# A 31-tap depthwise convolution inside a two-block model: two taps change engine, and the weight stream changes order

## What is computed

```python
u = h @ w_pw1 + b_pw1
a, gt = jnp.split(u, 2, axis=-1)
u = a * jax.nn.sigmoid(gt)
u = lax.conv_general_dilated(u, w_dw[:, None, :], window_strides=(1,),      # 31 taps, one filter a channel
    padding=[(15, 15)], dimension_numbers=("NWC", "WIO", "NWC"), feature_group_count=1024) + b_dw
u = jax.nn.silu(layernorm(u, ln_g, ln_b))
return u @ w_pw2 + b_pw2
```

## Time and profile before

| | |
|---|---|
| time, median of 3 runs | 1968.42 us (1966.68 to 1971.39) |
| span of the profiled execution | 1969.0 us |
| convolution's taps on TensorE | 121.8 to 168.9 us |
| first pw2 matmul | 184.1 us |
| busy: PE, DVE, ACT, POOL | 1889.2, 1201.8, 953.6, 542.5 us |

### The profile page before, as it was taken

How to read it: one execution, slowest core, us unless ns; L and a number is a source line. 1 busy time by engine, 2 the same in 40 slices (tenths; PEclk the granted TensorE clock), 3 DMA queues, 4 the chain that set the end, 5 groups by cost and what they waited for, 6 DMA issues and landing times.

```text
span 1969.0 us, 36121 instructions
## 1 busy us (share of the span) xinstructions
PE 1889.2 (96%) x14718; PEld 1668.6 (85%) x14718; DVE 1201.8 (61%) x2440; ACT 953.6 (48%) x1709; POOL 542.5 (28%) x685
## 2 busy tenths in 40 slices
PE   6999999999998989999998999999999999999998
PEld 4855778888886857899987989999999899989997
DVE  4989763233338575655579675685648876567473
ACT  4314532232224477544456474565555556456464
POOL 1320010000001533000021222747373322374736
PEclk9999999999999999899999999999999999999999
DMA  9335442222224254655544444455554544545551
GB/s 358 128 108 206 151 150 96 97 97 97 97 97 171 86 193 175 211 182 182 183 160 175 142 136 160 165 168 172 194 182 152 174 148 133 168 150 178 187 178 59
DMA packets 84548, 307.24 MB, mean 156 GB/s; under 512 B 9376, under 2 KB 10656, under 8 KB 84128
## 3 DMA queue, kind: packets, MB, share of 16 engines
q1 hardware_dynamic: 84384, 304.94, 45.4%
HBM read 303.86 MB, written 1.05 MB: 155 GB/s over the span
## 4 chain that ended last, share of the span: by engine, by line
PE 82%; DVE 10%; ACT 5%; DMA 2%; issue 1%; SPq 0%; POOL 0%; DVEq 0%; ACTq 0%
PE pb L540 18%; PE pb L542 18%; PE pb L541 18%; PE pb L513 7%; PE pb L514 6%; PE pb L519 6%; DVE wlo L1897 2%; DMA raw<-wstream 2%; ACT whi L1237 1%; PE pb L591 1%; DVE Y L2146 1%; PE pb L765 1%; PE pb L924 1%; PE pb L1108 1%; PE pb L1121 1%
## 5 line engine op out<-in xcount | busy, mean ns | idle before, releaser
L540 PE MATMUL pb<-Hh,whi 128*128 128x256 f32 (+1 forms) x2304 | 701.8, 305 | 1.8 <-DVE SM L2480 1.6
L542 PE MATMUL pb<-Hh,wlo 128*128 128x256 f32 (+1 forms) x2304 | 694.6, 301 | 0.0
L541 PE MATMUL pb<-Hl,whi 128*128 128x256 f32 (+1 forms) x2304 | 694.6, 301 | 0.0
L1237 ACT ACTIVATE whi<-raw 128x1024 fp32r<-128x1024 f32 x468 | 489.3, 1054 | 318.1 <-PE pb L542 171.2
L2855 POOL TENSOR_TENSOR wlo<-raw,whi 128x256 fp32r<-128x256 f32 x576 | 434.9, 790 | 734.9 <-ACT whi L1237 733.9
L1897 DVE TENSOR_TENSOR wlo<-raw,whi 128x1024 fp32r<-128x1024 f32 x324 | 421.2, 1305 | 344.1 <-ACT whi L1237 343.7
L540 PEld LDWEIGHTS pb<-Hh,whi 128*128 128x128 f32 x2304 | 441.9, 192 | 22.9 <-DVE SM L2480 2.5
L541 PEld LDWEIGHTS pb<-Hl,whi 128*128 128x128 f32 x2304 | 442.2, 192 | 15.0
L542 PEld LDWEIGHTS pb<-Hh,wlo 128*128 128x128 f32 x2304 | 442.0, 192 | 15.0
L513 PE MATMUL pb<-Hh,whi 128*128 128x256 f32 (+1 forms) x528 | 161.2, 327 | 4.6 <-ACT Hh L1311 3.2
L514 PE MATMUL pb<-Hh,wlo 128*128 128x256 f32 (+1 forms) x528 | 158.8, 322 | 0.0
(11 more groups left out here) (333 smaller groups left out, 2952.6 us busy)
## 6 DMA issues: line engine op xcount, KB each, us to landing
raw<-wstream SPq DMA_DIRECT2D x572, 512.0 KB, 3.5
X<-xin SPq DMA_DIRECT2D x2, 1024.0 KB, 7.7
out<-X SPq DMA_DIRECT2D x8, 128.0 KB, 1.8
CON<-consts SPq DMA_DIRECT2D x1, 926.0 KB, 8.6
VEC<-vecs SPq DMA_DIRECT2D x1, 662.0 KB, 9.5
CON<-consts SPq DMA_DIRECT2D x1, 147.0 KB, 3.8
VEC<-vecs SPq DMA_DIRECT2D x1, 88.0 KB, 2.0
```

Of the source, the lines that this page charges most:

```text
L540: e.matmul(dst, hi, xh, start=k == 0, stop=False)
L541: e.matmul(dst, hi, xl, start=False, stop=False)
L542: i = e.matmul(dst, lo, xh, start=False, stop=k == kt - 1)
L1237: e.activation(whi[:, s % NPIECE, :], raw[:, p % NRAW, :], ACT.Copy).then_inc(sig("act_hi", ("hi", p)), 1)
```

## The change

The weight stream gets pw2's first four tiles before C's modulation weights, C has three groups and N three (before: four and two). TensorE does taps 0 to 28 only. Taps 29 and 30 of its four tiles are made by VectorE as a part of each tile, with the negative shift as the start value (`part_taps`), and TensorE adds each part with one round of the plain diagonal. The sums for the shift come before the taps, the spread after tap 3. C's bites are after taps 2, 5, 8, 11, 14 and 17, the transpose of its row after tap 23, N's first bite after tap 26. No low half of pw1 is GpSimd's any more, but those of pieces 18 and 19 are. VectorE evicts three of TensorE's tiles and squares one, ScalarE evicts the fourth. The two idle matmuls ahead of the spread go. The scaled tiles get the buffers 5 to 7 under a name of their own (`ct`), parts the buffers 4 to 7.

```diff
+CONV_PE = 29
...
-CHUNKS = [(i, min(CHUNK, CONVW - i)) for i in range(0, CONVW, CHUNK)]
+CHUNKS = [(i, min(CHUNK, CONV_PE - i)) for i in range(0, CONV_PE, CHUNK)]
...
-MODS = {"S0": (0, 2, 2), "S1": (1, 2, 2), "C": (4, 4, 1), "N": (8, 2, 1), "F": (10, 3, 1), "A": (13, 3, 1),
+MODS = {"S0": (0, 2, 2), "S1": (1, 2, 2), "C": (4, 3, 1), "N": (7, 3, 1), "F": (10, 3, 1), "A": (13, 3, 1),
...
-    mod("C")
-    run([("conv_w_pw2", (0,), m * 128) for m in range(8)], FIRST, then=["N"])
+    run([("conv_w_pw2", (0,), m * 128) for m in range(8)], FIRST, then=["C", "N"])
...
-            if tag == "pw1":
-                return s > 5 and s % 3 == 0
+            if s in (tile_turn["pw1", 15] + 3, tile_turn["pw1", 15] + 4):
+                return True
...
+            bank("norm", ("stat", "cs"), ("root", "cs"))
+            w.wait_ge(*on("cv", 0))
+            quarters("cs", Y[:, 0:512], 512, True, False, ("zsum", "cs"))
+            w.wait_ge(*on("cv", 1))
+            quarters("cs", Y[:, 512:1024], 512, False, True, ("sums", "cs"))
             w.wait_ge(*on("pad"))
-            for ct in range(4):
-                w.wait_ge(*on("u", 4 + ct))
-            for i_ in range(CONVW + 1):
+            for i_ in range(CONV_PE):
                 c, q = i_ // CHUNK, i_ % CHUNK
                 w.wait_ge(*on("dg", c))
-                if i_ == CONVW:
-                    w.wait_ge(*on("shift"))
                 dg = DG[:, c % 3, :, :, :]
                 for ct in range(4):
+                    if i_ == 0:
+                        w.wait_ge(*on("u", 4 + ct))
                     for r in range(4):
                         rows = slice(32 * r, 32 * r + 32)
-                        src = U[rows, 4 + ct, :, i_:i_ + T] if i_ < CONVW else two(slots.at("shift")[rows, :])
-                        i = e.matmul(two(got[r][32 * ct:32 * ct + 32, :]), dg[rows, ct, q, :], src, start=i_ == 0, stop=i_ == CONVW)
-                if i_ == CONVW:
-                    i.then_inc(sig("pe_conv", ("dgused", c), *[("conv", r) for r in range(4)]), 1)
-                elif q == CHUNK - 1:
+                        i = e.matmul(two(got[r][32 * ct:32 * ct + 32, :]), dg[rows, ct, q, :], U[rows, 4 + ct, :, i_:i_ + T],
+                                     start=i_ == 0, stop=False)
+                if i_ == CONV_PE - 1 or q == CHUNK - 1:
                     i.then_inc(sig("pe_conv", ("dgused", c)), 1)
-                if i_ % 3 == 2 and i_ < 30:
+                if i_ == 24:
+                    feed("N")
+                if i_ % 3 == 2 and (i_ < 18 or i_ == 26):
                     bite(1)
-                    if i_ == 29:
-                        mod_tr("mods")
-                if i_ == 8:
-                    bank("norm", ("stat", "cs"), ("root", "cs"))
-                    w.wait_ge(*on("cv", 0))
-                    quarters("cs", Y[:, 0:512], 512, True, False, ("zsum", "cs"))
-                    w.wait_ge(*on("cv", 1))
-                    quarters("cs", Y[:, 512:1024], 512, False, True, ("sums", "cs"))
-                if i_ == 13:
+                if i_ == 23:
+                    mod_tr("mods")
+                if i_ == 3:
                     w.wait_ge(*on("root", "cs"))
                     widen("cs", 512, ("shift",), ring="norm")
...
+            for ct in range(4):
+                w.wait_ge(*on("part", ct))
+                for r in range(4):
+                    rows = slice(32 * r, 32 * r + 32)
+                    i = e.matmul(got[r][32 * ct:32 * ct + 32, :], con("blocks", p0=32 * r, p1=32 * r + 32),
+                                 slots.at(("part", ct))[rows, :], start=False, stop=True)
+            i.then_inc(sig("pe_conv", *[("conv", r) for r in range(4)]), 1)
+
+
             norm_sums(2, False, False)
             norm_sums(3, False, False)
             bite(1)
-            for k in range(4, 8):
-                norm_sums(k, False, k == 7)
-            bite(1)
+            for k in (4, 7, 6, 5):
+                norm_sums(k, False, k == 5)
+            bite(2)
             part[0] = 0
             r = slots.at(("root", "cv"))
-            widen("cv", 512, ("ctm", 7), r=r[:, 0:128], idle=2)
+            widen("cv", 512, ("ctm", 7), r=r[:, 0:128])
             widen("cvm", 512, ("ct", 7), r=r[:, 128:256])
...
-            hi_to(("pw1", 15), 1)
             row(1, "C")
-            hi_to(("pw1", 15), 4)
-            for k in range(2, 8):
+            conv_square(2)
+            conv_square(3)
+            w.wait_ge(*on("conv", 3))
+            e.activation(Y[:, 7 * 512:8 * 512], slots.at(("conv", 3)), ACT.Identity, bias=vec("conv_b_dw", 7)).then_inc(
+                sig("act_ev", ("fin", 7)), 1)
+            for k in (4, 7, 6):
...
+            def part_taps(ct):
+                t = buf(1.02, "part", ("part", ct), ("conv", 3))
+                w.wait_ge(*on("shift"))
+                w.wait_ge(*on("u", 4 + ct))
+                for i in range(CONV_PE, CONVW):
+                    if i > CONV_PE:
+                        w.wait_ge(*on("tap", 4 + ct, i - 1))
+                    points = [("tap", 4 + ct, i)] + ([("part", ct)] if i == CONVW - 1 else [])
+                    e.scalar_tensor_tensor(out=two(t), in0=U[:, 4 + ct, :, i:i + T], scalar=vec("conv_w_dw", i * 8 + 4 + ct),
+                                           in1=two(slots.at("shift") if i == CONV_PE else t), op0=ALU.mult, op1=ALU.add).then_inc(
+                        sig("dve_conv", *points), 1)
 
             tap(20)
             shift(0)
             tap(len(taps))
             shift(2)
             shift(3)
-            lo_to(("pw1", 15), 2)
+            for ct in range(4):
+                part_taps(ct)
             mod_add("C")
-            for r in range(4):
-                w.wait_ge(*on("conv", r))
-                e.tensor_scalar(Y[:, (4 + r) * 512:(5 + r) * 512], slots.at(("conv", r)), vec("conv_b_dw", 4 + r), None,
-                                ALU.add).then_inc(sig("dve_y", ("fin", 4 + r)), 1)
-
             mod_scale(0, 1, 2, 1, 0.0)
-            lo_to(("pw1", 15), 4)
+            for k in (4, 6, 5):
+                y = Y[:, k * 512:(k + 1) * 512]
+                w.wait_ge(*on("conv", k - 4))
+                e.tensor_scalar(y, slots.at(("conv", k - 4)), vec("conv_b_dw", k), None, ALU.add).then_inc(sig("dve_y", ("fin", k)), 1)
+            t = buf(1, "sq", ("sq", "cv", 5), ("sums", "cv"))
+            w.wait_ge(*on("fin", 5))
+            e.tensor_tensor(t, y, y, ALU.mult).then_inc(sig("dve_acc", ("sq", "cv", 5)), 1)
...
-                if c == 3:
-                    lo_to(("pw1", 15), 0)
                 for u in slots.take(0, "dg", ("dg", c), ("dgused", c)):
                     w.wait_ge(*u)
                 dg = DG[:, c % 3, :, :, :]
                     i = e.tensor_tensor(dg[:, ct, 0:n, :],
                                         con("blocks").rearrange("p (o m) -> p o m", o=1).broadcast_to((128, n, 32)),
                                         taps[:, :, 4 + ct:5 + ct].broadcast_to((128, n, 32)), ALU.mult)
-                if n < CHUNK:
-                    i = e.tensor_scalar(dg[:, :, n, :], con("blocks").rearrange("p (o m) -> p o m", o=1).broadcast_to((128, 4, 32)),
-                                        -1.0, None, ALU.mult)
                 i.then_inc(sig("pool_dg", ("dg", c)), 1)
+            lo_to(("pw1", 15), 4)
```

More of the change, by code:

```diff
@@ L335, in build @@
         scratch(1, row=[0], sq=[1, 2, 3], acc=[4], t=[5, 6, 7], s=[8, 9, 10])
+        scratch(1.02, part=[4, 5, 6, 7])
+        scratch(1.06, ct=[5, 6, 7])
         scratch(1.1, sq=[1, 2, 3, 0], acc=[4], accb=[5], accc=[6], xz=[7, 10], root=[8, 9])
@@ L787, in tensor @@
                     norm_sums(1, False, False)
-            feed("N")
+            for ct in range(4):
[5 more added lines that the diff above has]
+            i.then_inc(sig("pe_conv", *[("conv", r) for r in range(4)]), 1)
             norm_sums(2, False, False)
@@ L1351, in conv_square @@
             def conv_square(k):
-                t = buf(1, "sq", ("sq", "cv", k), ("sums", "cv") if k == 7 else ("xsum", "cv", k))
+                t = buf(1, "sq", ("sq", "cv", k), ("xsum", "cv", k))
                 w.wait_ge(*on("fin", k))
@@ L1360, in scalar @@
                 sig("act_root", ("root", "cs"), ("rec", "cs")), 1)
-            t = buf(1, "s", "shift", ("conv", 3), ("fin", 3))
+            t = buf(1, "s", "shift", ("fin", 3), *[("tap", 4 + ct, CONV_PE) for ct in range(4)])
             w.wait_ge(*on("spread", "cs"))
-            e.activation(t, slots.at(("spread", "cs")), ACT.Copy).then_inc(sig("act_ev", ("shift",)), 1)
+            e.activation(t, slots.at(("spread", "cs")), ACT.Copy, scale=-1.0).then_inc(sig("act_ev", ("shift",)), 1)
             conv_square(0)
             conv_square(1)
-            hi_to(("pw1", 15), 1)
             row(1, "C")
-            hi_to(("pw1", 15), 4)
-            for k in range(2, 8):
+            conv_square(2)
[4 more added lines that the diff above has]
+            for k in (4, 7, 6):
```

(6 more changed lines are left out.)

## The result

Six timed executions of the changed kernel have a median of 1986.14 us (1979.48 to 1987.47), six of the kernel before beside them 1969.91 (1966.68 to 1973.77). The ratio is 1.0069, 95% interval 1.0052 to 1.0085, so the change costs 0.0069 x 1970 = 13.6 us. The forecast was +7.6: the direction and the wait came as predicted, the size did not, and the time lies above the range.

What follows compares the result with a forecast made beforehand. TensorE, busy 96% of the span, was taken to bound the kernel; taps ending 14.8 us later less a tail gain of 7.2 made +7.6 on 1968.4, so 1976.0 us, range 1963.5 to 1981.

Steps and rivals of the forecast that it cites:

- The wait: TensorE's third bite, behind tap 8, waits 15.7 us for weights C5, whose buffer piece 18's low half holds.
- Kept out, let in: GpSimd, arriving during VectorE's running taps, is kept out until the first shift ends at about 139.2, then alternates with VectorE.
- let in at once: Rival, chance 0.22: GpSimd enters VectorE's tap chain without delay, C5 lands at 144.8, +2.3 us, 1970.7 us.
- Kept out through the shifts: Rival, chance 0.17: GpSimd enters only at VectorE's first gap, 163.1; C5 at 173.9, +31.4 us, 1999.8 us.
- After the wait: TensorE from third bite to end of taps: 30.2 us of work plus 3.4 lost to half clock; taps end +14.8 us.
- The tail: From the last tap to pw2's first matmul: 10.1 us instead of 15.2, if N's last bites are not late.
- The tail's gain of 7.2 us: Behind the taps: 5.1 us from an earlier pw2 start, plus 2.1 from pw2's first matmuls no longer at half clock.
- VectorE: free, as said: VectorE's 5 us of idle time pay for its part taps; with the wait it ends at 173.9 and is not last.
- the forecast's 164.5 against 168.1: Without a wait, TensorE's taps would end near 164.5 and VectorE's part taps last, at 168.1.

Runs made afterwards that it cites:

- the first experiment: The changed kernel, but GpSimd makes the low halves of pieces 18 and 19 before its fourth DG chunk; 1973.56 us, ratio 1.0009 to the kernel before.
- the stream order only: The kernel before with only the new weight stream, groups and bites, VectorE making all four low halves between pw1's taps; 1971.24 us, ratio 0.9997.
- the taps' part only: The changed kernel with the old weight stream, old groups of C and N and old share of low halves; 1974.86 us, ratio 1.0009 to the kernel before.

## Why the prediction was right in kind and short in size

Times of the changed profile are given less 0.8 us here, since its pw1 ended that much later.

**The wait: right.** Forecast 15.7 us at the third bite behind tap 8, released by the DMA; measured 16.28, in both profiles. Taking the low halves out from behind DG chunk 3 took it away, and the other two ways of changing the same chain shortened it by 4.8 and 3.4.

**Kept out, let in: right, one instruction off.** I let GpSimd in at the end of the first shift, 139.2. It was let in at the end of the second, 140.66 - 0.8 = 139.9, so the change from shift to shift did not do it and the change from shift to tap did, in this kernel and in the one with a shift inside the taps. C5 was there at 151.66 - 0.8 = 150.9 instead of 150.1, and TensorE wanted it at 134.6 instead of 134.4: the 0.6 us by which the wait is longer. The Trainium skill ("SBUF — State Buffer", Who interferes with whom) has the loser wait for the other's whole instruction; waits of 6.65, 6.92 and 7.78 us beside taps of 0.66 span eight and more instructions, in every profile in which the chain ran on, so "let in at once" fell. "Kept out through the shifts", 0.17, fell too, since GpSimd got in without any gap of VectorE (its sum has a slip: 163.1 and 11.0 make 174.1, not 173.9).

**After the wait: the sum held, its terms did not.** Forecast 30.2 + 3.4 = 33.6, measured 185.84 - 151.66 = 34.2. The clock was at half from 137.7 to 154.7 (third column from the right), but nearly all of that lay in the wait, where it costs nothing:

```profile
137.65:154.72 17.07, 3.06 (x40) 0.71 (x41) 17.07 (x20) 1.23 (x2) 15.05 (x12) 0.50 0.16 49
```

Beside work stood 3.06 us, so 1.5 were lost in this execution and not 3.4. In the second profile of the changed kernel the half clock reached 5.03 us into the work, so 2.5 were lost:

```profile
152.12:157.15 5.03, 5.03 (x72) 1.44 (x73) 5.03 (x8) 0.00 (x0) 1.03 (x1) 0.50 0.57 207
```

Against that C6 and C7 came 1.46 us late (1.58 in the second profile), a second wait I had not looked for: behind a late C5 the next loads are late as well. Some 0.8 us in the six taps from 168.63 on stay unexplained; in the second profile the same taps take 6.59 us instead of 7.51.

**The tail: 0.7 long.** 10.8 us instead of 10.1. N's last pieces were late after all (0.93 at 195.64, 0.41 in the second profile), where I had put them 1.1 us ahead.

**The tail's gain of 7.2 us, read from one profile: this is the step that failed.** Up to here I am 2.2 us short: against the first profile of before the stage grew by 93.0 - 83.2 = 9.8, forecast 7.6. The other 3.7 come from that profile. My tail term of -7.2 took off a last bite at half clock that waited 2.66 us (15.2 us of tail) and 2.1 us for pw2's first matmuls at half clock. Both are the trace's, and both were read correctly. But in the later three profiles the tail is 13.7, 12.7 and 13.6 us, no half clock lies behind the last bite, and the stage is 3.7 us shorter. A change can't give back what most executions don't pay. Against those three the taps end 64.4 - 48.3 = 16.1 us later behind pw1 (forecast 14.8), and the tail gives back 13.4 - 10.8 = 2.6 us and not 7.2. So of the 5.9 us by which the stage's growth of 93.0 - 79.5 = 13.5 passes the forecast, 4.6 are this term and 1.3 the wait and what follows it. I had asked whether the clock would fall in the new tail, which cost an end of the range (5.1 instead of 7.2), and never whether it always falls in the old one.

This is shown for the stage, and less firmly for the whole kernel. The first profile was not slow as a whole: its span is 1969.0 us, 1.1 to 1.6 above the later three, because its pw1 ended 1.2 to 3.0 us earlier, and its mean granted clock of 0.991 lies among their 0.993, 0.990 and 0.991. Part of the stretches at half clock lie at other places in each execution: one at 182 to 188 us in the first profile, at 26 to 30 us in the second. And behind the fixed point the changed kernel has 1768.5 and 1767.5 us, the kernel before 1764.4 to 1766.4; no run tells chance from cause there.

**VectorE: free, as said, in this kernel.** Its parts ended at 172.7 (forecast 173.9), and it waited 8.25 us for TensorE. Without the wait it is the bound, as the forecast's 164.5 against 168.1 said: 2.06 us in the kernel with the low halves on VectorE. Going back to one tap ended that.

**Total.** 1986.1 instead of 1976.0: of the 10.1, 6.0 are the move (13.6 instead of 7.6). The kernel before was itself 1.5 us above its first three runs in the six (1969.9 against 1968.4), and the two medians differ by 16.2 where the ratio gives 13.6, which makes 2.6.

## What to carry to other kernels

When a step moves to another engine's queue, walk that queue from the step back to the last wait: two low halves, 9 us of GpSimd's work, cost this kernel some 12 of its 13.6 us because one wait for a consumer stood before them, and the buffer they held stood before every later weight. Before charging a stretch at low clock, or a wait of 1 to 3 us, as gain or loss, ask whether every execution has it; one profile can't tell, and three more moved my base by 3.7 us. Where VectorE was never idle here, the order of its own list decided when GpSimd got in: a shift moved by six taps shortened the wait by 4.8 us.

## What the runs showed of the hardware that was not expected

- GpSimd's new operation is kept out by a chain of SCALAR_TENSOR_TENSOR for as long as it runs (6.0 to 7.9 us in twelve profiles; the one exception of 2.07 is where a shift broke the chain), yet once let in the two alternate, 0.9 to 1.17 us each. One start was let in at once: in the first experiment a low quarter at 118.85 took 1.24 us inside a chain, 1.23 us after GpSimd's quarter before it had ended. What sets that apart is open.
- The change from TENSOR_TENSOR to SCALAR_TENSOR_TENSOR let GpSimd in (140.66 in the changed kernel, 136.53 with the shift inside the taps). The one between two TENSOR_TENSOR shifts did not, nor did the one from tap to shift (139.46 and 135.93).
- The granted clock fell to half in pauses of 2.66 us (first profile of before) and not in ones of 2.08 and 1.99 at the same place, but it did behind a pause of 2.06 us in the kernel with the low halves on VectorE (at 169.9, for 3.4 us) and behind one of 2.28 with the stream order only (at 124.8, for 3.4 us), and not behind one of 2.10 with the taps' part only. Behind long pauses the half clock reached 3.06 and 5.03 us into the work (16.28 us, the changed kernel's two profiles), 4.1 (11.45 us) and 6.1 (12.83 us): half of that was lost, and the longest pause did not cost most.
